# Attention and pooling of a two-layer hybrid trunk: masks ahead of scores, narrower value products, another order of small steps

## The reference

```
h = rms_norm(x, ffn_norm); x = x + 0.5 * swiglu(h, wg, wu, wd)
x = x + hybrid_mixer(rms_norm(x), ...)        # layer 0
x = x + pool_mixer(rms_norm(x), ...)          # layer 1
# in the first mixer, scale = 64 ** -0.5, q and k normed, rotary on 16 of 64:
p_cmp = softmax(where(blk_end <= t, q @ kc * scale, NEG)) * any_valid
p_slc = softmax(where(kpos <= t, q @ ks * scale, NEG))   # all 8 blocks are chosen
p_win = softmax(where(causal and diff < 512, q @ kw * scale, NEG))
o = g0 * (p_cmp @ vc) + g1 * (p_slc @ vs) + g2 * (p_win @ vw)
conv: v = gate_c * u; o_b = gate_b * (w2 * v + w1 * shift(v, 1) + w0 * shift(v, 2))
out = concat([o, o_b]) @ w_out
# in the second mixer, for each of the 4 groups of 256 features:
out = ((sliding_mean(h) - h) @ w[group]) * pool_scale
```

## Time and profile before

| | us |
|---|---|
| median of 3 runs (lowest, highest) | 1823.35 (1821.74, 1824.59) |
| profiled execution | 1822.51 |
| its span, first to last instruction | 1820.6 |
| TensorE busy, products | 1791.4 |
| VectorE busy | 861.1 |
| ScalarE busy | 605.6 |
| GpSimd busy | 103.7 |
| mean granted clock of TensorE | 0.998 |

### The profile page before, as it was taken

How to read it: one execution, slowest core, us unless ns; L and a number is a source line. 1 busy time by engine, 2 the same in 40 slices (tenths; PEclk the granted TensorE clock), 3 DMA queues, 4 the chain that set the end, 5 groups by cost and what they waited for, 6 DMA issues and landing times.

```text
span 1820.6 us, 22353 instructions
## 1 busy us (share of the span) xinstructions
PE 1791.4 (98%) x8196; PEld 1473.6 (81%) x8196; DVE 861.1 (47%) x1124; ACT 605.6 (33%) x894; POOL 103.7 (6%) x91
## 2 busy tenths in 40 slices
PE   8999999999999999999999999999999999999999
PEld 6888888877867877888888888888888878888887
DVE  5544443366777735444443344444433454444322
ACT  5233232235336534333322233333222433233211
POOL 0500000012000001000000000000001100000000
PEclk9999999999999999999999999999999999999999
DMA  5333343224320012333333323333432223333331
GB/s 174 93 100 96 93 122 95 82 81 99 87 69 13 1 41 87 102 94 92 103 114 100 98 81 93 103 92 99 117 95 65 76 86 99 92 99 109 108 99 47
DMA packets 321362, 163.68 MB, mean 90 GB/s; under 512 B 13893, under 2 KB 320041, under 8 KB 321322
## 3 DMA queue, kind: packets, MB, share of 16 engines
q1 hardware_dynamic: 321130, 163.08, 31.2%
q10 hardware_dynamic: 192, 0.08, 0.0%
HBM read 161.04 MB, written 2.10 MB: 90 GB/s over the span
## 4 chain that ended last, share of the span: by engine, by line
PE 94%; DVE 4%; ACT 1%; issue 1%; DMA 0%; SPq 0%; POOL 0%; DVEq 0%; ACTq 0%
PE ps_s L538 20%; PE ps_s L540 20%; PE ps_s L539 19%; PE ps_y L540 9%; PE ps_y L538 9%; PE ps_y L539 9%; PE ps_aux L863 2%; DVE w_lo L1407 1%; PE ps_y L846 1%; PE ps_s L816 1%; PE ps_s L814 1%; DVE xg_lo L1425 1%; ACT w_hi L1018 1%; PE ps_aux L860 1%; DMA x_in<-in_x 0%
## 5 line engine op out<-in xcount | busy, mean ns | idle before, releaser
L1407 DVE TENSOR_TENSOR w_lo<-raw,w_hi 128x1024 fp32r<-128x1024 f32 (+2 forms) x279 | 367.6, 1318 | 738.8 <-ACT w_hi L1018 738.3
L538 PE MATMUL ps_s<-xg_hi,w_hi 128*128 128x512 f32 x1608 | 631.9, 393 | 8.8 <-DVE xg_lo L1425 5.6
L540 PE MATMUL ps_s<-xg_hi,w_lo 128*128 128x512 f32 x1608 | 626.0, 389 | 0.0
L539 PE MATMUL ps_s<-xg_lo,w_hi 128*128 128x512 f32 x1608 | 625.9, 389 | 0.0
L1018 ACT CAST w_hi<-raw 128x1024 fp32r<-128x1024 f32 (+2 forms) x279 | 312.1, 1119 | 596.3 <-PE ps_s L540 302.5
L538 PEld LDWEIGHTS ps_s<-xg_hi,w_hi 128*128 128x128 f32 x1608 | 301.8, 188 | 78.0 <-DVE xg_lo L1425 8.3
L539 PEld LDWEIGHTS ps_s<-xg_lo,w_hi 128*128 128x128 f32 x1608 | 301.9, 188 | 64.3 <-issue 2.4
L540 PEld LDWEIGHTS ps_s<-xg_hi,w_lo 128*128 128x128 f32 x1608 | 301.8, 188 | 63.4
L538 PE MATMUL ps_y<-act_hi,w_hi 128*128 128x512 f32 x704 | 274.3, 390 | 0.7 <-DVE w_lo L1407 0.7
L540 PE MATMUL ps_y<-act_hi,w_lo 128*128 128x512 f32 x704 | 274.0, 389 | 0.0
L539 PE MATMUL ps_y<-act_lo,w_hi 128*128 128x512 f32 x704 | 274.0, 389 | 0.0
(11 more groups left out here) (310 smaller groups left out, 1081.8 us busy)
## 6 DMA issues: line engine op xcount, KB each, us to landing
raw<-in_ffn_w_gate SPq DMA_DIRECT2D x88, 512.0 KB, 3.9
raw<-in_ffn_w_up SPq DMA_DIRECT2D x88, 512.0 KB, 3.9
raw<-in_ffn_w_down SPq DMA_DIRECT2D x64, 704.0 KB, 4.5
...
```

Of the source, the lines that this page charges most:

```text
L538: mm(bank, hi, x_hi, start=first, stop=False, **kw)
L539: mm(bank, hi, x_lo, start=False, stop=False, **kw)
L540: return mm(bank, lo, x_hi, start=False, stop=last, **kw)
L1407: tt(w_lo[:, n % 2, 0:size], raw[:, n % 4, 0:size], f32(w_hi[:, n % 2, 0:size]), ALU.subtract).then_inc(lo_ready, 1)
```

## The change

- `scores`: the masks of both branches are written first, then the key products are added. `scores_c`: one mask of 128 columns for all four chunks, then eight products.
- `values`: for the top block only the second half (128 queries) is multiplied; the zeros and GpSimd's writing of them go.
- The factor 1/8 goes into the query's norm (ScalarE's root with scale 1 and 64 * EPS). `maxima` then writes negated maxima at once; the negation instruction goes.
- Compressed branch: VectorE subtracts the maxima from the scores into `prob_c`, ScalarE takes one exp of all 128 columns, VectorE sums the result (`reduce_sum`).
- Start of attention: VectorE makes `maxima(0, 0)`, `maxima_c(0, 0)`, `maxima(0, 1)`, `scales(0, 0)` before it frees the last projection's bank; the rest of the last convolution tile follows in steps 1 and 2.
- The attention's output has tensors of its own, `o_hi` and `o_lo` (in the room of tensors that are done before attention). `tile_order` goes: `take_x(2, d)` and `xg_low(2, d)` follow each tile of the output projection.
- `band_product`: no zero product; the first band product starts the bank. The zeroing of `mask_b` goes.
- VectorE adds the pooled tiles one ahead of their `xg_low`. `first_pair` shares blocks 0 to 3 and then finishes unit 0 before unit 1. The squares of the last norm are added on VectorE (`sum_squares`) with the splits of units 2 and 3 between; `total_stat` stands before block 6 of unit 2, not block 2.

Some words that came with the change name turned banks shared by ScalarE and VectorE; `take_probs` is not in the diff. The core of the diff (declarations and repeated edits left out, eight spaces of indent taken off):

```diff
-        for k in range(KD):
+        def block_of(m, k):
+            return three(ps_s[:, 2 * m, :], w_hi[:, (n + m) % 2, k * P:(k + 1) * P],
+                         w_lo[:, (n + m) % 2, k * P:(k + 1) * P], tile_of(xg_hi, k), tile_of(xg_lo, k), k == 0, k == KD - 1)
+        for k in range(KD // 2):
             pe.wait_ge(xg_lo_ready, KD * XG_OF[5] + k + 1)
             for m in range(2):
-                last_mm = three(ps_s[:, 2 * m, :], w_hi[:, (n + m) % 2, k * P:(k + 1) * P], w_lo[:, (n + m) % 2, k * P:(k + 1) * P],
-                                tile_of(xg_hi, k), tile_of(xg_lo, k), k == 0, k == KD - 1)
-                if k == KD - 1:
-                    last_mm.then_inc(unit_done, 1)
+                block_of(m, k)
+        for m in range(2):
+            for k in range(KD // 2, KD):
+                if m == 0:
+                    pe.wait_ge(xg_lo_ready, KD * XG_OF[5] + k + 1)
+                last_mm = block_of(m, k)
+            last_mm.then_inc(unit_done, 1)
...
         for br in range(2):
             bank = ps_s[:, 2 * (s % 2) + br, :]
-            mm(bank[:, 0:wide], query, k_hi[:, br, g, 0:wide], start=True, stop=False)
-            mm(bank[:, c * P:width], ident_b[:, :], mask_b[:, 0:P], start=False, stop=False)
-            last_mm = mm(bank[:, 0:wide], query, k_lo[:, br, g, 0:wide], start=False, stop=True)
+            mm(bank[:, c * P:width], ident_b[:, :], mask_b[:, 0:P], start=True, stop=False, skip_group_check=True)
+        for br in range(2):
+            bank = ps_s[:, 2 * (s % 2) + br, :]
+            mm(bank[:, 0:wide], query, k_hi[:, br, g, 0:wide], start=False, stop=False, skip_group_check=True)
+            last_mm = mm(bank[:, 0:wide], query, k_lo[:, br, g, 0:wide], start=False, stop=True,
+                         skip_group_check=True)
...
         for c in range(NQ):
             bank = ps_stat[:, c * NCP:(c + 1) * NCP]
             query = q_parts[:, g, c * P:(c + 1) * P]
-            mm(bank, query, kc_hi[:, g, :], start=True, stop=False)
-            mm(bank, ident_b[:, :], mask_b[:, P + c * NCP:P + (c + 1) * NCP], start=False, stop=False)
-            last_mm = mm(bank, query, kc_lo[:, g, :], start=False, stop=True)
+            mm(bank, query, kc_hi[:, g, :], start=False, stop=False)
+            last_mm = mm(bank, query, kc_lo[:, g, :], start=False, stop=c == NQ - 1)
...
-            for k in range(2 * half_pair + 2):
-                last_mm = mm(bank, v_t[:, br, k * P:(k + 1) * P], probs[:, br, k, :, :], start=False,
-                             stop=br == 1 and k == 2 * half_pair + 1)
+            for k in range(2 * half_pair + 1):
+                mm(bank, v_t[:, br, k * P:(k + 1) * P], probs[:, br, k, :, :], start=False, stop=False)
+            k = 2 * half_pair + 1
+            last_mm = mm(bank[:, P:2 * P], v_t[:, br, k * P:(k + 1) * P], probs[:, br, k, 1, :], start=False, stop=br == 1)
...
-        mm(bank, mask_b[:, 0:P], mask_b[:, 0:P].unsqueeze(1).to_broadcast([P, NQ, P]), start=True, stop=False)
         for b in range(NQ):
             cols_ = band(g, b)
-            last_mm = mm(bank[:, b * P:b * P + cols_.shape[1]], z_t[:, b, d * P:(d + 1) * P], cols_, start=False,
-                         stop=b == NQ - 1)
+            last_mm = mm(bank[:, b * P:b * P + cols_.shape[1]], z_t[:, b, d * P:(d + 1) * P], cols_, start=b == 0,
+                         stop=b == NQ - 1, skip_group_check=True)
         last_mm.then_inc(band_done, 1)
...
                 exps(0, 0)
                 exps_c(0, 0)
-            if u == 3:
-                act.wait_ge(ob_ready, b + i + 1)
-                copy(tile_of(ob_hi, b + i), work2[:, :]).then_inc(ob_hi_ready, 1)
+                exps(0, 1)
+            if u == 3 and not b:
+                convolved_high(i, work2[:, :])
+    def convolved_high(j, at):
+        act.wait_ge(ob_ready, j + 1)
+        copy(tile_of(ob_hi, j), at).then_inc(ob_hi_ready, 1)
...
-        act.wait_ge(c_negmax_ready, 2 * j + g + 1)
-        for c in range(NQ):
-            last = nc.scalar.activation(prob_c[:, c, :], ps_stat[:, c * NCP:(c + 1) * NCP], ACT.Exp,
-                                        bias=small_c[:, 0, c:c + 1], scale=DH ** -0.5,
-                                        accum_out=small_c[:, 1, c:c + 1])
-        last.then_inc(c_exp_done, 1)
+        act.wait_ge(c_shifted, 2 * j + g + 1)
...
                 take_probs(j, s - 1)
-            if not (last and s == 7):
+            if not (last and s == 7) and not (first and s == 0):
                 exps(j, s + 1)
+            if first and s == 1:
+                convolved_high(3, work[:, 0, :])
...
         split(U_OUT + d + 2)
-        if d < KD - 1:
-            take_x(2, d, R_FFN + 8 if d >= LATE else None)
-    act.wait_ge(unit_done, U_OUT + KD)
-    for d in range(LATE):
-        xg_high(d, R_FFN + 8)
-    take_x(2, KD - 1, R_FFN + 8)
+        take_x(2, d, R_FFN + 8)
...
+    def sum_squares(ffn):
+        dve.wait_ge(sq_ready, KD * 5)
+        then(tt(sq_tiles[:, 0:4, :], sq_tiles[:, 0:4, :], sq_tiles[:, 4:8, :], ALU.add))
+        split(U_FFN[ffn] + 2)
+        then(tt(sq_tiles[:, 0:2, :], sq_tiles[:, 0:2, :], sq_tiles[:, 2:4, :], ALU.add))
+        tt(ss[:, :], sq_tiles[:, 0, :], sq_tiles[:, 1, :], ALU.add).then_inc(ss_step, KD)
+        split(U_FFN[ffn] + 3)
...
                     maxima(0, 0)
                     maxima_c(0, 0)
-                scaled(n, p, work2[:, :], i=i)
-                if not b:
+                    maxima(0, 1)
+                    scales(0, 0)
+                    scaled(n, p, work[:, 0, :])
+                else:
+                    scaled(n, p, work2[:, :], i=i)
                     split(n + 2, i)
-                dve.wait_ge(proj_scaled, p + 1 + 4 * i)
-                dve.wait_ge(conv_step, 4 * b + 4 + 4 * i)
-                tt(work2[:, :], work2[:, :], y, ALU.mult).then_inc(ob_ready, 1)
-                dve.wait_ge(ob_hi_ready, j + 1)
-                tt(tile_of(ob_lo, j), work2[:, :], f32(tile_of(ob_hi, j)), ALU.subtract).then_inc(ob_lo_ready, 1)
+                    convolved(b, i, j, p, work2[:, :])
+                    convolved_low(j, work2[:, :])
             if extra and u == 0:
                 extra[0]()
+    def convolved(b, i, j, p, at):
+        dve.wait_ge(proj_scaled, p + 1 + 4 * i)
+        dve.wait_ge(conv_step, 4 * b + 4 + 4 * i)
+        tt(at, at, vt[:, :], ALU.mult).then_inc(ob_ready, 1)
+    def convolved_low(j, at):
...
         dve.wait_ge(qk_done, 8 * j + s + 1)
-        nc.vector.reduce_max(m[:, 8:10], ps_s[:, 2 * (s % 2):2 * (s % 2) + 2, 0:width], AX_X).then_inc(max_step, 1)
-        dve.wait_ge(max_step, 8 * j + s + 1)
-        ts(m[:, 0:2], m[:, 8:10], -DH ** -0.5, None, ALU.mult).then_inc(negmax_ready, 1)
+        nc.vector.reduce_max(m[:, 0:2], ps_s[:, 2 * (s % 2):2 * (s % 2) + 2, 0:width], AX_X,
...
         nc.vector.reduce_max(small_c[:, 4, :], ps_stat[:, 0:NQ * NCP].rearrange("p (c n) -> p c n", n=NCP),
                              AX_X).then_inc(c_max_step, 1)
         dve.wait_ge(c_max_step, 2 * j + g + 1)
-        ts(small_c[:, 0, :], small_c[:, 4, :], -DH ** -0.5, None, ALU.mult).then_inc(c_negmax_ready, 1)
+        tt(prob_c[:, :, :], ps_stat[:, 0:NQ * NCP].rearrange("p (c n) -> p c n", n=NCP),
+           small_c[:, 4, :].unsqueeze(2).to_broadcast([P, NQ, NCP]), ALU.subtract).then_inc(c_shifted, 1)
     def scales_c(j, g):
         dve.wait_ge(c_exp_done, 2 * j + g + 1)
+        nc.vector.reduce_sum(small_c[:, 1, :], prob_c[:, :, :], AX_X).then_inc(c_total_step, 1)
...
-    for d in (*range(LATE), KD - 1):
         xg_low(2, d, R_FFN + 8)
     run_ffn(1, 2, 3, R_FFN + 16)
     run_ffn(2, 3, 4, R_MIX + KD)
...
     split(U_TAIL + 8)
+    add_pooled(0)
+    add_pooled(1)
+    xg_low(5, 0, R_FFN + 24)
+    add_pooled(2)
+    xg_low(5, 1, R_FFN + 24)
     split(U_TAIL + 9)
-    for d in range(KD):
+    for d in range(3, KD):
         add_pooled(d)
-        xg_low(5, d, R_FFN + 24)
+        xg_low(5, d - 1, R_FFN + 24)
+    xg_low(5, KD - 1, R_FFN + 24)
```

104 lines of the change are left out of this document (48 added, 56 removed).

## The result

The changed kernel takes 1798.32 us (median of 4 runs, 1797.34 to 1798.53) beside 1822.55 us of the kernel before: the ratio is 0.9865, 95% interval 0.9848 to 0.9882. The forecast was 1802 us (1794 to 1810). 21.2 us were expected and 24.2 came.

The account below looks back on a forecast made before the run. TensorE, busy 98% of the span, was taken to bound the kernel. Attention 8.0, start 2.5, projection 2.4 and pooling 8.3 make 21.2 us; 1822.51 less that is 1801.3, with 0.84 to the median 1802 us (range 1794 to 1810).

Parts of the forecast that it names:

- Attention, what TensorE is spared: Attention: value products, masks and compressed scores together spare TensorE 13.6 us, 1.7 us for each of eight rounds.
- Value products 7.5: Attention: 64 value instructions become half as wide, 0.117 us spared each, 7.5 us.
- Masks 4.8: Attention's wide scores: masks standing together ahead of the key products spare 0.15 us, 32 times, 4.8 us.
- Compressed scores 1.3: Attention's compressed scores: eight products and one mask take 0.91 us instead of 1.07, eight times, 1.3 us.
- Attention, 8.0 of them: Attention: VectorE takes over as bound, rounds go from 14.32 to 13.25 us, so only 8.0 of 13.6 us count.
- my two signs: Attention: rounds of 13.3 us would show the forecast right, rounds under 12.8 us that TensorE keeps the bound.
- the first rival: Attention: TensorE keeps the bound, 13.6 us gained instead of 8.0, so 1796.5 us; chance 0.17.
- Start, 2.5 us: Start of attention: maxima and first scaling ahead of the convolution bring TensorE's third-step transposes 2.5 us earlier; ends 0 and 5.3.
- Projection, 2.4 us: Output projection into feed-forward: TensorE's two waits for xg_lo, 2.3 us, and 0.1 for restarts go; other end 1.5.
- Tile 7's cover: Behind the output projection: tile 7, ready 4.5 us after the unit, is covered by 4.8 us of other tiles' products.
- Pooling, 8.3 us: Pooling into last feed-forward: zero products 1.8 and waits with restarts 6.95, less 0.4 left standing; ends 5 and 9.
- Fourth rival: TensorE's new pauses in attention's rounds cost the clock, 27 us on top, 1829 us; chance 0.04.

Follow-up runs that it names:

- full_values: The changed kernel with the value products full width again (64 instructions of 256 columns in place of 128): 1804.49 us.
- padded: The changed kernel with compressed values and probabilities padded with zero rows from 32 to 128, so each value pair's first product has 128 rows: 1794.07 us.
- masks_between: The changed kernel with the mask products of the wide scores between the two key products again: 1799.94 us.
- negate_apart: The changed kernel with the maxima negated by a VectorE instruction of their own again: 1798.84 us.
- start_before: The changed kernel with the convolution's products ahead of the second maxima and the first scaling again, where attention starts: 1800.75 us.
- gpsimd_sums: The changed kernel with the last sum of squares on GpSimd again (seven adds), VectorE's splits unchanged: 1799.98 us.
- add_in_series: The changed kernel with VectorE's old order behind the pooling: both splits first, then each tile's add and xg_lo of the same tile: 1806.09 us.

## Why the prediction was right, and where it was not

The time was right within 3.7 us. The gain was short by 3.0, since the kernel before took 0.8 us less this time. By its own steps:

**Attention, what TensorE is spared** (13.6 us forecast). Value products 7.5: 6.6 measured. The narrow ones are as forecast (0.11 us); 256 columns in a running row take 0.222 us (597.11 - 593.56 over 16), 0.006 less than the chain's pieces gave. Masks 4.8: 2.5 measured. Inside the scores 0.18 us went, more than the 0.15 forecast; but ahead of the masks the transposes grew by 0.09, a term that the sum did not have. Compressed scores 1.3: they take 0.93 us where they took 1.07, 0.14 x 8 = 1.1, not tested alone; eight products at 0.11 and a mask of 0.058 make 0.94 and not the 0.91 that the sum had.

**Attention, 8.0 of them.** This step failed. VectorE did not take over: rounds of 13.09 us, and 12.6 on the mean with padding. I had read 13.2 us as VectorE's own length of a round because it stood only 1.11 us for ScalarE's copy. But the rest held waits too: 2.6 us in five waits for TensorE's scores and 2.6 us in six for the query's parts (before, 548 to 640 us). After (548 to 628 us) they are 0.3 us in one and 2.1 in five, while the wait for exps went from 1.4 to 2.7 us: the order of VectorE's work could move up when TensorE did. A round of 13.09 us alone lies between my two signs, 13.3 and under 12.8; full_values and padded decide it. The sum came out near by luck, two errors against each other: TensorE was spared less than I thought (about 10 of 13.6), and it lost nothing to VectorE in the running rounds, where the sum took off 5.6. So the first rival had the mechanism right and the size wrong, and its 1796.5 us lies nearer to 1798.3 than my 1802. The four parts undone one by one (full_values, masks_between, negate_apart, start_before) give 12.4 us in stretch 1 without the compressed scores, more than the 12.2 measured; how they overlap stays open.

**Start, 2.5 us:** 2.3, but not by the way forecast. The first pause came as forecast (1.7 for 2.0); the five pauses together are 3.6 us where two had been 3.8, so they gave next to nothing. What went is the stretch at 1.2 GHz behind the pause of 3.0 us, which the sum named only in its far end. Size right, step wrong.

**Projection, 2.4 us:** the waits' part is 2.8 (restarts 0.24 each, not 0.05), less the 0.6 that the place of the new buffers costs, which no row of before could show: 2.2, where the stretch has 2.1. Tile 7's cover held. The rule of the Trainium skill (SBUF — State Buffer, Who interferes with whom) that I weighed here did not come into play at this place, each `xg_lo` took 0.75 us; gpsimd_sums shows the conflict it describes, at the pooling.

**Pooling, 8.3 us:** 9.4. Zero products 1.8: 1.7. The waits, 6.3 us, went. Restarts, forecast at 0.13, cost 0.24 to 0.27: five times 0.25 makes 1.25 and not 0.65. The 0.4 that I left standing did not stand: after has no wait of TensorE there at all, and the granted clock is 1.00 throughout. That gives 1.7 + 6.3 + 1.25 = 9.25. The sum on VectorE, which I had only priced as a cost, is worth 2.0 us by itself: it takes GpSimd's adds from beside `xg_lo`. The order of the products in `first_pair` and the place of `total_stat` were not tested alone.

**Fourth rival.** It did not happen in the change, but it is real: add_in_series. My argument against it, waits of up to 1.8 us that left the clock alone, held for that row and not for the pauses of add_in_series.
